# First unit in seven pieces of one to four rows, small tables behind x, products of zeros ahead of the first piece

## What is computed

```python
u = rmsnorm(h, g_mix[i])          # x * rsqrt(mean(x * x) + eps) * g
proj = u @ w_in[i]                # 2048 x 10784
q, k, v, z, xbc, dt_raw, g_a, g_s = jnp.split(proj, offsets, axis=-1)
q = apply_rope(q, positions)
```

## Time and profile before

| | before |
|---|---|
| timed runs | 2740.9, 2742.9, 2743.19 us; median 2742.9 |
| span of the profiled execution | 2741.4 us |
| busy: PE, DVE, ACT | 2706.7, 1961.1, 1411.7 us |
| weight pieces in all | 940 |

### The profile page before, as it was taken

One profiled execution on the slowest core, in us unless ns is written; L12 is line 12 of the kernel. 1 busy time (PEld: TensorE's weight loads), 2 busy tenths in 40 slices (PEclk: granted clock), 3 DMA queues, 4 the chain that ended last, 5 costly groups with the idle time before them and its releaser, 6 DMA issues.

```text
span 2741.4 us, 41654 instructions
## 1 busy us (share of the span) xinstructions
PE 2706.7 (99%) x16606; PEld 2376.5 (87%) x16606; DVE 1961.1 (72%) x2946; ACT 1411.7 (51%) x2092; POOL 105.6 (4%) x197
## 2 busy tenths in 40 slices
PE   8999999999999999999999999999999999999998
PEld 7878888888888888888888889998888888888887
DVE  7558778757677776677766678877787775677765
ACT  6455556544455554455545552247665553455543
POOL 1320000000000000000000000000000000000000
PEclk9999999999999999999999999999999999999999
DMA  7557556555568888888856556873455556555554
GB/s 241 153 179 226 175 184 200 185 184 186 200 218 288 286 283 288 294 283 283 284 200 211 179 175 228 311 264 121 140 190 185 190 197 190 182 193 185 185 195 143
DMA packets 168915, 581.58 MB, mean 212 GB/s; under 512 B 20129, under 2 KB 26993, under 8 KB 168209
## 3 DMA queue, kind: packets, MB, share of 16 engines
q1 hardware_dynamic: 152368, 526.06, 58.3%
q0 software_dynamic: 16208, 52.85, 5.2%
q10 hardware_dynamic: 144, 0.01, 0.0%
HBM read 535.06 MB, written 43.09 MB: 211 GB/s over the span
## 4 chain that ended last, share of the span: by engine, by line
PE 92%; DVE 4%; ACT 2%; DMA 1%; issue 1%; SPq 0%; POOL 0%; DVEq 0%; ACTq 0%; POOLq 0%
PE PS L956 91%; DVE wl L1921 1%; DMA raw<-in_w_in 1%; ACT wh L1379 1%; PE PS L1294 0%; ACT SX1b L1379 0%; DVE SQA L1921 0%; DVE H L1921 0%; ACT SX1a L1379 0%; DVE TA L1929 0%; DVE SX1b L2067 0%; DVE Z L1921 0%; DMA raw<-in_w_down 0%; DVE CC L1929 0%; ACT TB L1379 0%
## 5 line engine op out<-in xcount | busy, mean ns | idle before, releaser
L1921 DVE TENSOR_TENSOR wl<-raw,wh 128x1024 fp32r<-128x1024 f32 (+3 forms) x888 | 1039.4, 1195 | 464.2 <-ACT wh L1379 462.6
L1379 ACT ACTIVATE wh<-raw 128x1024 fp32r<-128x1024 f32 (+3 forms) x888 | 893.8, 1030 | 502.4 <-PE PS L956 401.4
L956 PE MATMUL PS<-CHt,wh 128*128 128x512 f32 x2816 | 885.9, 395 | 0.0
L956 PE MATMUL PS<-BIGt,wh 128*128 128x512 f32 (+1 forms) x2816 | 755.0, 356 | 1.5 <-issue 0.6
L956 PE MATMUL PS<-AHt,wh 128*128 128x512 f32 (+1 forms) x2080 | 636.5, 386 | 17.0 <-DVE wl L1921 16.9
L956 PEld LDWEIGHTS PS<-CHt,wl 128*128 128x128 f32 x2816 | 529.0, 188 | 124.8
L956 PE MATMUL PS<-CHt,wl 128*128 128x256 f32 x2816 | 553.5, 278 | 0.0
L956 PEld LDWEIGHTS PS<-BIGt,wl 128*128 128x128 f32 x2304 | 434.9, 189 | 79.0 <-issue 0.2
L956 PE MATMUL PS<-BIGt,wl 128*128 128x256 f32 x2304 | 497.8, 279 | 0.0
L956 PEld LDWEIGHTS PS<-BIGt,wh 128*128 128x128 f32 x2816 | 434.1, 190 | 6.3 <-issue 3.8
L956 PEld LDWEIGHTS PS<-AHt,wl 128*128 128x128 f32 x1952 | 368.5, 189 | 80.2 <-issue 0.7
(11 more groups left out here) (311 smaller groups left out, 1633.7 us busy)
## 6 DMA issues: line engine op xcount, KB each, us to landing
raw<-in_w_up SPq DMA_DIRECT2D x264, 512.0 KB, 4.9
raw<-in_w_in SPq DMA_DIRECT2D x196, 512.0 KB, 4.3
raw<-in_w_down SPq DMA_DIRECT2D x132, 512.0 KB, 4.3
raw<-in_w_gate SPq DMA_DIRECT2D x88, 512.0 KB, 5.4
raw<-in_w_down SPq DMA_DIRECT2D x56, 384.0 KB, 3.6
PKR<-in_w_in SPq DMA_DIRECT2D x36, 512.0 KB, 5.4
parked_halves<-PKH POOLq DMA_DIRECT2D x36, 512.0 KB, 5.9
parked_halves<-PKL POOLq DMA_DIRECT2D x36, 512.0 KB, 7.1
```

What stands on the lines that cost most here:

```text
L956: return e.matmul(o, l, r, start=start, stop=stop, skip_group_check=True)
L1379: return e.activation(o, x, f, **k)
L1921: return e.tensor_tensor(o, x, y, op)
```

## The change

Unit 0 is cut in seven pieces of 1, 1, 2, 4, 4, 2 and 2 rows (`FIRST`), both its weights and x, so the 16 rows stay the same. All later pieces keep their size and get numbers three higher. The plan begins with seven pairs of `seed` and `split`, each with a further `fetch`. The four phases of `sum_x` wait five steps of the side lane. ACT issues x pieces 0 and 1 behind its load of `g_mix`; SP issues weights 0, 1 and 2, then x 2 and 3, weight 3, x 4, 5 and 6. POOL fills `SQA` with zeros first, then the margins and `NEGT`, and waits for the last x piece before it issues the small tables. Some of these share semaphores: positions with `CV` (and with x, when it is loaded again much later), the mask with the rows. PE multiplies the zeros in `SQA` three times (`WARM`), 512 columns of float32 each, into bank 7, before its first piece. DVE's first copy into `SQA` waits until PE has done piece 0.

```diff
+FIRST = (1, 1, 2, 4, 4, 2, 2)
+WARM = 3
@@ pieces
-            subs += [(n, ms, k, min(step, u.nk - k)) for k in range(0, u.nk, step)]
+            if n == 0:
+                subs += [(n, ms, sum(FIRST[:j]), c) for j, c in enumerate(FIRST)]
+            else:
+                subs += [(n, ms, k, min(step, u.nk - k)) for k in range(0, u.nk, step)]
@@ make_plan
-    for s in range(4):
+    for s in range(len(FIRST)):
         plan.append(("seed", s, 0))
         plan.append(("split", s, 0))
-        ns += 1
+        plan.append(("fetch", nf, 0))
+        nf, ns = nf + 1, ns + 1
-    side.extend([stage("sum_x", 0, 4)])
+    side.extend([stage("sum_x", 0, 4, len(FIRST) - 2)])
@@
+    def load_x(e, i):
+        k, c = sum(FIRST[:i]), FIRST[i]
+        src = a["xT"][P * k:P * (k + c), :].rearrange("(t p) n -> p t n", p=P)
+        e.dma_start(H[:, k:k + c, :], src).then_inc(x_in[i], 16)
@@ sync_program
-        load_x(0)
...
-            if s < 3:
-                load_x(s + 1)
+            if s in (2, 3):
+                for i in ((2, 3), (4, 5, 6))[s - 2]:
+                    load_x(e, i)
@@ pool_program
+        e.memset(SQA[:, :, :], 0.0).then_inc(filled.sem)
...
-        e.memset(NEGT[:, :], NEG).then_inc(neg_made.sem)
-        e.wait_ge(x_in[1], 16)
+        e.memset(NEGT[:, :], NEG).then_inc(filled.sem)
+        e.wait_ge(x_in[-1], 16)
@@ tensor_program
+        e.wait_ge(filled.sem, 1)
+        still = SQA[:, :, :].rearrange("p a b -> p (a b)")
+        for _ in range(WARM):
+            mm(PS[:, 7, :], SQA[:, 0, 0:P], still)
@@ scalar_program
+        for i in range(2):
+            load_x(e, i)
         e.wait_ge(pad.sem, 1)
@@ seed, on ACT and on DVE
-            for k in range(4 * i, 4 * i + 4):
+            for k in range(sum(FIRST[:i]), sum(FIRST[:i + 1])):
@@ gather
                 if j:
                     e.wait_ge(nrm_pe.sem, j)
+                else:
+                    e.wait_ge(sub_done.sem, 1)
@@ rotary, on DVE
-                e.wait_ge(cv_in, 16)
...
-                e.wait_ge(pos_in, 16)
+                e.wait_ge(cv_in, 32)
@@ attn1, on DVE
-                if t == 0:
-                    e.wait_ge(mask_in, 16)
```

More of the change, by code:

```diff
@@ L633, in hybrid_block_kernel @@
     raw_in = [dma(f"raw{i}") for i in range(NRAW)]
-    g_in, cv_in, mats_in, mask_in, row_in, pos_in = (dma(n) for n in ("g_mix", "cv", "mats", "mask", "row", "pos"))
-    x_in = [dma(f"x{i}") for i in range(4)]
+    g_in, cv_in, mats_in, row_in = (dma(n) for n in ("g_mix", "vecs_positions_then_x_again", "mats", "row_and_mask"))
+    x_in = [dma(f"x{i}") for i in range(len(FIRST))]
     dist_out, head_out, query_out, cbi_in, bm_in, p_in, w2_in = (
@@ L638, in hybrid_block_kernel @@
     xc_in = dma("blocks")
-    neg_made = steps("neg_made")
+    filled = steps("filled")
     w1_in = [dma("w1k"), dma("w1v")]
@@ L709, in hybrid_block_kernel @@
     cst_out, csb_in = dma("sums_by_head"), [dma("sums_lo"), dma("sums_hi")]
-    x_again = dma("x_again")
+    x_again = cv_in
     full_a = {"U1": steps("full_u1")}
@@ L755, in hybrid_block_kernel @@
     LN_READ = {0: "mean", 5: "rs", 8: "sp"}
+    def load_x(e, i):
+        k, c = sum(FIRST[:i]), FIRST[i]
+        src = a["xT"][P * k:P * (k + c), :].rearrange("(t p) n -> p t n", p=P)
+        e.dma_start(H[:, k:k + c, :], src).then_inc(x_in[i], 16)
     def sync_program(e):
-        def load_x(i):
-            src = a["xT"][512 * i:512 * (i + 1), :].rearrange("(t p) n -> p t n", p=P)
-            e.dma_start(H[:, 4 * i:4 * i + 4, :], src).then_inc(x_in[i], 16)
-        load_x(0)
         for kind, s, _ in plan:
@@ L810, in pool_program @@
     def pool_program(e):
+        e.memset(SQA[:, :, :], 0.0).then_inc(filled.sem)
         for z in Z:
             e.memset(z[:, :, 0:30], 0.0).then_inc(pad.sem)
-        e.memset(NEGT[:, :], NEG).then_inc(neg_made.sem)
-        e.wait_ge(x_in[1], 16)
+        e.memset(NEGT[:, :], NEG).then_inc(filled.sem)
+        e.wait_ge(x_in[-1], 16)
         e.dma_start(CV[:, 16:], a["vecs"][:, 16:]).then_inc(cv_in, 16)
-        e.dma_start(PI[:, :], a["positions"].partition_broadcast(P)).then_inc(pos_in, 16)
+        e.dma_start(PI[:, :], a["positions"].partition_broadcast(P)).then_inc(cv_in, 16)
         e.dma_start(M7[:, 0:2, :].rearrange("p a b -> p (a b)"), a["mats"][:, 0:2 * P]).then_inc(mats_in, 16)
@@ L820, in pool_program @@
         e.dma_start(ROW[:, :], a["rows"].partition_broadcast(P)).then_inc(row_in, 16)
-        e.dma_start(MK1[:, :], a["mask1"]).then_inc(mask_in, 16)
+        e.dma_start(MK1[:, :], a["mask1"]).then_inc(row_in, 16)
         def lookup():
             rel = a["rel"].tensor
-            e.wait_ge(neg_made.sem, 1)
+            e.wait_ge(filled.sem, 2)
             for j in range(2):
@@ L1463, in rotary @@
                 af(COS[:, :], RO[:, 0, 1, :], ACT.Sin).then_inc(rot_a.sem)
-                e.wait_ge(row_in, 16)
+                e.wait_ge(row_in, 32)
                 af(alog, alog, ACT.Exp).then_inc(rot_a.sem)
@@ L1986, in rotary @@
         def rotary(_, ph):
-            if ph == 0:
-                e.wait_ge(cv_in, 16)
             ang, kk, r0 = RO[:, 0, 0, :], RO[:, 0, 1, :], RO[:, 1, 0, :]
@@ L2284, in ev_h @@
             if i == 0:
-                e.wait_ge(x_again, 32)
+                e.wait_ge(x_again, 64)
             if i >= 8 and i < 24:
```

## The result

The change made the kernel slower by 4.6 us: 2748.03 us median (2745.05 to 2750.08), against 2743.4 (2740.9 to 2745.94) for the kernel before beside it on the same chip. The ratio is 1.0015, with an interval of 1.0009 to 1.0022: inside the 0.2% that the prediction called "the same", and clear of 1. The forecast was +0.85 us and 2743.8. The sign was right, the size was not, and the time lies above the range. Half a microsecond of that is the kernel before itself, which took 2742.9 in the runs that the forecast starts from.

The account below looks back on a forecast made before the run. PE bounds the kernel, but DVE paces it up to the matmul at 58.44. Norm 1.7 us later, half paid by the vanished 0.85 us wait: 2742.9 + 0.85 gives 2743.8 us; own range 2742.5 to 2745, 8-in-10 range 2740.0 to 2746.0.

Parts of the forecast that it names:

- the matmul at 58.44: PE matmul after a 0.85 us wait for DVE's low half; forecast to move to 59.3, the change's whole worth.
- Seeds and lows: ACT's and DVE's splits at the start: low halves 0 to 6 forecast to end from 6.2 to 18.5.
- Landings of pieces 8 and 9: Weight transfers queued with all the small tables, forecast to land at 20.2 and 21.5 us.
- The list behind low 9: DVE's work from low half 9 to the last sum of squares: 9.2 us, ending at 32.9.
- rival B: Tables and pieces share DMA better, DVE runs without a pause; norm matmul 1.6 us early, 2740.5 us; chance 0.28.
- PE at the norm: PE reaches the norm matmul at 29.4, waits 3.5 us for DVE's last sum, starts 1.7 us later than before.
- The wait at 58.44: PE's 0.85 us wait for DVE's low half disappears and pays for half of what the norm costs.
- PE at full rate behind the new wait: After waiting 3.5 us at the norm, PE was taken to lose nothing to a halved clock.
- rival D: The wait at the norm cools PE to half rate, costing 1.9 us: +2.75 in all, 2745.7 us; chance 0.16.
- Zeros: Three products before PE's first piece: may save 1.9 us or delay it up to 0.6; forecast worth nothing.
- rival E: Zeros don't raise the clock or end late; unit 0 ends up to 1.9 us later, same total; chance 0.03.
- Rival C: The whole start is won, 6.4 us less, 2736.5 us; needs the last sum by 26; chance 0.05.

Follow-up runs that it names:

- fourteen kernels: The kernel before, the kernel after and the twelve follow-up kernels made by editing one or the other; one profiled execution each.
- 4: Kernel before plus the zeros alone: memset of `SQA`, three products of zeros, the gather's wait on `sub_done`; ratio 0.9996.
- 5: Kernel after with POOL issuing the small tables behind low half 9 instead of the last x piece; 2747.59 us, ratio 1.0017.
- 7: Kernel before with the sums of squares two steps later in the plan, behind low half 6 instead of 4; 2745.75 us, ratio 1.0009.
- 10: Kernel after with squares three steps earlier and the norm one piece earlier, POOL's wait for the tables unchanged; 2746.25 us, ratio 1.0013.
- 8: Kernel after with squares two steps earlier (behind low half 7) and the tables issued behind low half 8; 2743.26 us, ratio 0.9999.
- 11: Kernel after without zeros, squares two steps earlier (behind low half 7), tables issued behind x piece 3; 2744.81 us, ratio 1.0003.
- 6: Kernel after with POOL issuing the tables behind x piece 3 instead of the last x piece; 2747.53 us, ratio 1.0017.
- 3: Kernel after without the three products of zeros (`WARM = 0`); 2749.6 us, ratio 1.0020.

## Why the prediction was right, and where it wasn't

**What the change is worth is what it moves the matmul at 58.44: right.** Later waits kept their size and shifted together, by 4.98 to 5.00 us. None of them changed with the numbers of the pieces.

**Seeds and lows: right up to old piece 3.** Low halves ended at 5.7, 7.2, 8.7, 11.8, 15.8, 17.2 and 18.6 (forecast 6.2, 7.1, 8.6, 11.7, 15.5, 17.0, 18.5). The waits of PE for lows 2, 3 and 4 are there, 0.40, 1.44 and 0.90 us.

**Landings of pieces 8 and 9: 1.1 us short.** Forecast 20.2 and 21.5, measured 21.3 and 22.6. ACT's and DVE's timelines of the kernel after:

```profile
21.38 1.06 ACT L1392 ACTIVATE wh<-raw 128x1024 fp32r<-128x1024 f32 x1 [3.25 <-DMA raw<-in_w_in]
```

```profile
22.48 2.50 DVE L1936 TENSOR_TENSOR wl<-raw,wh 128x1024 fp32r<-128x1024 f32 x2 [2.76 <-ACT wh L1392]
...
33.75 0.42 DVE L1936 TENSOR_TENSOR SQA<-SQA 128x256 f32<-128x256 f32 x1
```

The mechanism was right: ACT waits for the DMA behind the tables, and DVE idles 2.76 us. The term mis-sized is the rate. I took the 389 GB/s of 7 to 20; the kernel after moved 381 from 7 to 13 and 361 from 13 to 20. Piece 8's 6.32 MB were through by about 19.9 in place of 19.1, which is 0.7 of the 1.1; the rest is in the last step to landing. The Trainium skill's fit that the prediction set beside its landings ("DMA: Bandwidth & Descriptors", section on the anatomy of one DMA) is given there for transfers that GpSimd issues, and these are issued by ACT and SP. In the kernel after, 128 KB took 2.4 us for weights and 3.6 for x. The list behind low 9 took 9.3 us (forecast 9.2), so the last sum ended at 34.17 for 32.9, and rival B, which has DVE without a pause, is out.

**PE at the norm.** It reached it at 30.05 (forecast 29.4) and waited 4.27 us (3.5). The forecast took the shift of the norm matmul as 1.7 us, from 31.23, which is its weight load; from the matmul itself, at 31.46, it is 2.86.

**The wait at 58.44 went, as forecast.** It was worth 1.04, not 0.85. I had taken the idle time that the profile lists behind the modelled end of the product at 57.19. The next product was due 0.24 after that one's start, at 57.43, and started at 58.44: 1.01. With this, the shift without half rate is 2.86 - 1.04 = 1.82 for my 0.85.

**The step that failed: PE at full rate behind the new wait.** The forecast put the cost of half rate behind the 3.5 us at the norm at nothing and left it to rival D, with 0.16. D is what happened, and it makes 3.16 of the 4.98 us. I had read "full rate after 2.45" from the first product alone, one group of rows too short. PE's timeline of the kernel *before*, a few rows on:

```profile
144.77 0.50 PE L956 MATMUL PS<-AHt,wh 128*128 128x512 f32 x1 [2.45 <-DVE wl L1921]
...
145.34 0.63 PE L956 MATMUL PS<-AHt,wh 128*128 128x512 f32 x2
...
146.04 1.02 PE L956 MATMUL PS<-AHt,wh 128*128 128x512 f32 x2
```

The clock fell 1.3 us after work had resumed, and products ran at half rate until 149.9; the windows of that kernel give 0.52 from 146 to 148. With these rows, half rate behind a wait of 3.5 us would have been the more likely case, and the forecast D's. It would not have been a sure one: this same wait of 2.45 us is in all fourteen kernels, and the clock fell behind it in ten of the profiled executions and stayed full in four (4, 5, 7 and 10). Here the Trainium skill ("TensorE: Matmul & The Clock Gate", section on HAM oscillation) had it right where my reading of the row did not; this case shows the drop after 1.81 us as well, though not after every wait of that size. The price was low too: I charged the 1.9 us of the kernel's start. The stretch at half rate lasted 7 us here, and cost 3.16.

**Zeros (rival E): half right.** In the profiled execution they ran at half rate for all their 5.49 us, ended at 6.8 and held the first piece, whose low half was ready at 5.7, for 1.1 us. The clock was up when they ended. Both came to nothing, as forecast, since PE waits at the norm anyway. "If that wait went, they would be worth 1.9" was not borne out: in 8 that wait is gone and the zeros are in, in 11 it is gone and they are not, and the marks are 0.07 us apart (their tables differ too).

**Rival C and the structure.** The start was won, 2.4 us and full rate, and stayed without value, since DVE, and not PE, sets the low half at 58. The forecast said so for the last sum; 8 and 11 show it for the scaling, in 8 with a wait of DVE for a transfer in it.

## What to carry to other kernels

A change that starts an engine earlier is worth what the slower list beside it allows: find the next place where that engine waits for the other one (here the low half at 58, set by DVE's scaling), and ask whether the change shortens *that* list. When a step is moved behind others on one engine, a wait appears on the engine that needs it, and on TensorE its price is the delay of what waits plus, in some executions, the half clock behind it. Unused products put into the wait are a cheap test of the second part. When you ask whether a wait costs clock, read the trace for several us behind the first product, not the first product alone, and look at the same wait in more than one execution.

## What the runs showed of the hardware

- **The same wait may or may not halve the clock.** In the first 155 us the clock fell to half after waits of 1.81 (in 7), 1.82 (in 6), 2.77, 3.99, 4.27 and 4.44 us, and not after 1.89 (in 6), 1.69 (in 11), 1.65, 1.62, 1.43 and shorter ones. Behind the wait of 2.45 us at 144.77, which all fourteen kernels have, it fell in ten profiled executions and stayed full in four. One of the four is that of 7, in PE's timeline and in the windows:

```profile
146.89 0.50 PE L956 MATMUL PS<-AHt,wh 128*128 128x512 f32 x1 [2.46 <-DVE wl L1921]
```

```profile
148.00:150.00 2.00, 1.96 (x12) 1.47 (x10) 0.67 (x4) 1.26 (x4) 0.00 (x0) 1.00 0.86 305
```

- In 6, a wait of 1.89 us at full rate is followed by one of 1.82 with a fall:

```profile
12.37 0.50 PE L964 MATMUL PS<-AHt,wh 128*128 128x512 f32 x1 [1.89 <-DVE wl L1936]
...
17.25 0.50 PE L964 MATMUL PS<-AHt,wh 128*128 128x512 f32 x1 [1.82 <-DVE wl L1936]
...
18.98 1.05 PE L964 MATMUL PS<-AHt,wh 128*128 128x512 f32 x2
```

- Late in the kernel before, PE's timeline has a wait of 1.77 us with full rate behind it and one of 1.67 us with a fall; the windows behind each give the clock (third column from the right). The second of these waits, 1.67 to 1.70 us in the others, had a fall behind it in seven of the fourteen executions.

```profile
1682.41 0.33 PE L956 MATMUL PS<-GCM,W2C 64*64 64x64 f32 x4 [1.77 <-DVE GCM L1925]
...
1862.21 0.65 PE L956 MATMUL PS<-PT2a,VC 15*64 15x128 f32 x8 [1.67 <-ACT PT2a L1379]
```

```profile
1684.00:1687.00 3.00, 3.00 (x28) 3.00 (x27) 3.00 (x8) 1.80 (x2) 0.00 (x0) 1.00 0.57 172
...
1862.00:1864.00 2.00, 1.06 (x10) 0.83 (x11) 2.00 (x7) 2.00 (x7) 0.00 (x0) 0.75 0.35 55
```

- The fall can come with the first product or after 0.6 to 1.3 us of work at full rate (0.6 in the kernel after at 149.77, 0.8 behind the 2.77, 1.3 in the kernel before at 144.77).
- In these first 155 us the clock stayed at half for 3.0 to 7.0 us. That was not ordered by the wait's length: 7.0 after 4.27, but some 4.6 after 4.44.
- At the start of a program the granted clock of the windows doesn't show the half rate: it reads 1.00 from 3 to 7 us in the kernel after, while the zeros take 5.49 us for six instructions of 512 columns, 0.91 each, where full rate would give 0.46 (an estimate, twice the 0.23 of 256 columns that the prediction takes from the earlier trace rows). In later stretches it reads 0.50 to 0.58.
- Products of zeros raised the clock: the first product behind them took 0.40 to 0.50 us in the kernel after and in 4, against 0.77 without them in 3.
- 1.08 MB of tables issued by POOL between two weight pieces made the piece behind them land 5.5 us after its issue, against 3.2 without them (the kernel after and 5).
